# Branch gates of the second block: from two plain tile products to the seven-product scheme, with weight sums made by accumulating DMAs

## What is computed

```python
def hybrid_mixer(h, w_in, w_diff_o, w_sb_o, w_moba_o, w_out, ...):
    proj = h @ w_in                      # h: 256 positions x 1024
    (dq, dk, dv, sq, sk, sv, mq, mk, mv, g_diff, g_sb, g_moba) = jnp.split(proj, offsets, axis=-1)
    a_out = ... diff_attention ...       # softmax, two maps per head
    b_out = ... stick_breaking_attention ...
    c_out = ... moba_attention ...       # softmax
    merged = (jax.nn.sigmoid(g_diff) * (a_out @ w_diff_o)
              + jax.nn.sigmoid(g_sb) * (b_out @ w_sb_o)
              + jax.nn.sigmoid(g_moba) * (c_out @ w_moba_o))
    return merged @ w_out
```

## Time and profile before

| | us |
|---|---|
| median of 3 runs | 3351.42 |
| lowest and highest run | 3348.72, 3353.06 |
| the profiled execution | 3349.66 |
| its span in the trace | 3347.8 |

### The profile page before, as it was taken

The page is one execution under the profiler, slowest core; times in us unless marked ns, Lnnn a source line. Parts: engine busy times, 40 slices in busy tenths (PEclk is TensorE's granted clock), DMA queues, the critical chain, the costliest instruction groups (busy, mean ns, idle before and its releaser), DMA issues.

```text
span 3347.8 us, 54286 instructions
## 1 busy us (share of the span) xinstructions
PE 3288.6 (98%) x22634; PEld 2943.0 (88%) x22634; DVE 2120.8 (63%) x4269; ACT 682.9 (20%) x1675; POOL 187.1 (6%) x140
## 2 busy tenths in 40 slices
PE   7999999999999999999999999999999999999999
PEld 5888755788888888878999999988999999988999
DVE  3579654456654157765789685744486886644685
ACT  2101442012211011242122111124211212032211
POOL 0000000005443400000000000000000000000000
PEclk9999999999999999999999999999999999999999
DMA  6243001223223443503554445633444444633443
GB/s 241 77 176 126 26 26 63 101 87 126 84 84 111 153 150 126 186 32 114 190 187 160 170 166 182 176 132 114 140 175 164 164 169 160 191 125 121 156 164 127
DMA packets 67397, 453.76 MB, mean 136 GB/s; under 512 B 7377, under 2 KB 11857, under 8 KB 15057
## 3 DMA queue, kind: packets, MB, share of 16 engines
q1 hardware_dynamic: 66384, 446.09, 37.7%
q10 hardware_dynamic: 768, 4.20, 0.7%
HBM read 445.02 MB, written 1.05 MB: 133 GB/s over the span
## 4 chain that ended last, share of the span: by engine, by line
PE 91%; DVE 6%; ACT 2%; DMA 1%; issue 1%; SPq 0%; DVEq 0%; ACTq 0%
PE bank L1353 64%; PE bank L1041 14%; DVE conv_sum L2847 3%; PE bank L1666 2%; PE bank L1153 1%; PE bank L1183 1%; PE bank L1106 1%; PE bank L1091 1%; PE bank L1208 1%; PE bank L1713 1%; PE bank L1298 1%; DMA weight_ring<-w_o 1%; PE bank L1276 0%; PE bank L1503 0%; PE bank L1287 0%
## 5 line engine op out<-in xcount | busy, mean ns | idle before, releaser
L1353 PE MATMUL bank<-normed,weight_ring 128*128 128x128 f32 (+1 forms) x5472 | 764.6, 295 | 5.3 <-ACT normed L1883 1.5
L1353 PEld LDWEIGHTS bank<-normed,weight_ring 128*128 128x128 f32 x5472 | 707.7, 192 | 42.4 <-issue 7.6
L1353 PE MATMUL bank<-normed,mixer_small 128*128 128x128 f32 (+1 forms) x3040 | 387.2, 281 | 0.0
L1353 PEld LDWEIGHTS bank<-normed,mixer_small 128*128 128x128 f32 x3040 | 366.4, 192 | 4.9
L1353 PE MATMUL bank<-region_a,weight_ring 128*128 128x128 f32 (+1 forms) x2128 | 294.4, 293 | 0.7 <-DVE region_a L2804 0.6
L1353 PEld LDWEIGHTS bank<-region_a,weight_ring 128*128 128x128 f32 x2128 | 272.1, 192 | 11.7 <-issue 2.0
L1353 PE MATMUL bank<-turned,weight_ring 128*128 128x256 f32 (+1 forms) x944 | 199.0, 353 | 0.0
L1353 PEld LDWEIGHTS bank<-turned,weight_ring 128*128 128x128 f32 x944 | 163.6, 190 | 18.4
L1041 PE MATMUL bank<-turned,weight_ring 128*128 128x256 f32 x768 | 178.8, 382 | 0.0
L1353 PE MATMUL bank<-region_a,mixer_small 128*128 128x128 f32 (+1 forms) x1232 | 161.8, 282 | 0.0
L1041 PEld LDWEIGHTS bank<-turned,weight_ring 128*128 128x128 f32 x768 | 140.8, 190 | 22.5 <-issue 5.0
(11 more groups left out here) (340 smaller groups left out, 4883.8 us busy)
## 6 DMA issues: line engine op xcount, KB each, us to landing
weight_ring<-w_ada SPq DMA_DIRECT2D x48, 1024.0 KB, 5.8
weight_ring<-w_up SPq DMA_DIRECT2D x44, 1024.0 KB, 4.8
weight_ring<-w_f1up SPq DMA_DIRECT2D x44, 1024.0 KB, 4.8
weight_ring<-w_f2up SPq DMA_DIRECT2D x44, 1024.0 KB, 4.8
weight_ring<-w_gt SPq DMA_DIRECT2D x32, 1024.0 KB, 4.8
weight_ring<-w_qk SPq DMA_DIRECT2D x24, 1024.0 KB, 4.8
weight_ring<-w_v SPq DMA_DIRECT2D x20, 1024.0 KB, 5.9
weight_ring<-w_pj SPq DMA_DIRECT2D x16, 1024.0 KB, 4.8
```

Of the source, the lines that this page charges most:

```text
L1353: mm = nc.tensor.matmul(bank[u.bank][:, pair.columns(p)], lhs(k), rhs(k), start=begins and p in pair.opens and k == 0, stop=ends and p in ...
```

## The change

The 24 gate tiles become 12 pairs by the seven-product scheme. Each pair's seven products are dealt to the same four filler halves: products 1 and 2; 7 and 6; 5; 3 and 4. The first two halves fill bank 6, the last two bank 7. ACT no longer copies whole tiles but one quarter of the pair (`gate_first`); DVE puts the pair together in its loop (`gate_mix`, placed behind `exponent` and ahead of `store`) and writes it to `gates2`. Since the weight sums are made by adds alone, the signs of the scheme are moved: the activation sums are partly negated, each pair's second tile comes out negated, and the sigmoid of it is taken with scale -1. The activation sums are four DVE operations ahead of the loop. The weight sums are made by DMAs that POOL issues: one load of three quarters of the block from HBM into an entry of `wsum`, and four adds.

```diff
+GATE_PARTS = [(1, 2), (7, 6), (5,), (3, 4)]
+GATE_PAIRS = 12
@@ PE, a half of a filler
+                    if name == "gt2":
+                        x, n = 2 * (g % 2) + half, GATE_PAIRS * l + g // 2 + 1
+                        if g == 0 and half == 0:
+                            pe.wait_ge(turned_ready, T.next(turned_ready, 4))
+                        if x == 1:
+                            pe.wait_ge(gate_s1_s3, 32 * n)
+                            pe.wait_ge(gate_s2, 16 * n)
+                        if x == 3:
+                            pe.wait_ge(gate_s4, 16 * n)
+                        seven(b, g // 2 % SUM_RING, plan.pairs[name][g // 2], KD // 2, gate_act, None, gsums_used,
+                              True, True, l, wsum, None, None, GATE_PARTS[x], 4, (2, 0, 1))
+                        return
...
-                    if name == "sv2":
-                        mm = value_part(u, b, g % 2, range(half * n, half * n + n))
-                    else:
-                        mm = product(bank[u.bank][:, 0:SEQ], b, g % 2 * KD + half * n, hnorm2, 0, SEQ, n, half * n,
-                                     half == 0, half == 1)
+                    mm = value_part(u, b, g % 2, range(half * n, half * n + n))
@@ ACT
-                def gate_copy(g):
-                    u = plan.units["gt2"][g]
-                    full_bank(u, 0, l)
-                    a_(gates2[g // KD][:, g % KD, :], bank[u.bank][:, 0:SEQ], ACT.Copy).then_inc(bank_free[u.bank], 1)
+                def gate_first(g):
+                    units = plan.units["gt2"]
+                    full_bank(units[g], 0, l)
+                    if g >= 4:
+                        emptied(act, units[g - 4], l)
+                    a_(one_gate[:, g // 2 % 2, :], bank[units[g].bank][:, 0:P], ACT.Copy).then_inc(one_copied, 1)
...
-                        x = gates2[b][:, m:m + n, :]
-                        a_(x, x, ACT.Sigmoid).then_inc(gates2_ready, 1)
+                        x, minus = gates2[b][:, m:m + n:2, :], gates2[b][:, m + 1:m + n:2, :]
+                        a_(x, x, ACT.Sigmoid)
+                        a_(minus, minus, ACT.Sigmoid, scale=-1.0).then_inc(gates2_ready, 1)
@@ DVE, ahead of the loop
+                v.tensor_tensor(minus_t1, b11, b12, ALU.subtract).then_inc(turned_ready, 1)
+                v.scalar_tensor_tensor(minus_t2, minus_t1, -1.0, b22, ALU.mult, ALU.subtract).then_inc(turned_ready, 1)
+                v.tensor_tensor(hn[:, half:KD, P:2 * P], b22, b12, ALU.subtract).then_inc(turned_ready, 1)
+                v.scalar_tensor_tensor(hn[:, 0:half, P:2 * P], minus_t2, -1.0, b21, ALU.mult, ALU.subtract
+                                       ).then_inc(turned_ready, 1)
@@ DVE, in the loop
+                    gate_mix(n - 1)
                     if n >= 1 and n % 2 == 0:
                         store(n // 2 - 1)
...
+                gate_mix(23)
                 store(11)
@@ POOL
+            for l in range(DEPTH):
+                u = plan.units["qk2"][-1]
+                pool.wait_ge(bank_full[u.bank], count(u, 0, l) + 1)
+                for j, b in enumerate(plan.blocks["gt2"]):
+                    n = GATE_PAIRS * l + j + 1
+                    quarters = weights["gt2"][l * N_BLOCKS["gt2"] + j]
+                    a21 = ring_t[:, b.slot * SLOT + 2 * w:b.slot * SLOT + 3 * w]
+                    s2, s4, s1 = (wsum[:, j % SUM_RING, i, :] for i in range(3))
+                    if n > SUM_RING:
+                        pool.wait_ge(gsums_used, n - SUM_RING)
+                    g.dma_start(wsum[:, j % SUM_RING].rearrange("p a c -> p (a c)"), quarters[:, 0:3 * w]
+                                ).then_inc(gate_loaded, 16)
+                    pool.wait_ge(slot_landed[b.slot], (count(b, 0, l) + 1) * 16)
+                    g.dma_start(a21, quarters[:, 0:w], accum_op=ALU.add).then_inc(gate_s1_s3, 16)
+                    pool.wait_ge(gate_loaded, 16 * n)
+                    g.dma_start(s1, quarters[:, 3 * w:4 * w], accum_op=ALU.add).then_inc(gate_s1_s3, 16)
+                    pool.wait_ge(gate_s1_s3, 32 * n)
+                    g.dma_start(s2, s1, accum_op=ALU.add).then_inc(gate_s2, 16)
+                    pool.wait_ge(gate_s2, 16 * n)
+                    g.dma_start(s4, s2, accum_op=ALU.add).then_inc(gate_s4, 16)
```

More of the change, by code:

```diff
@@ L272, in filler2 @@
         self.blocks[name][-1].after = self.units[name][-1]
+        if name == "gt2" and g % 2:
+            self.pairs.setdefault(name, []).append(Pair(self.units[name][-2:], P, False))
     def take_blocks(self, name, dram, n, cols, first=0):
@@ L868, in build @@
         gains_ready, resa_ready = sem("gains_ready"), sem("resa_ready")
+        gsums_used, gate_loaded, gate_s1_s3, gate_s2, gate_s4 = (sem(n) for n in (
+            "gsums_used", "gate_loaded", "gate_s1_s3", "gate_s2", "gate_s4"))
         qk_pair, swap_landed = sem("qk_pair"), [sem(f"swap{i}_landed") for i in range(2)]
@@ L1318, in attention1, with seven @@
                         turn(n + 1)
-            def seven(b, s, pair, n, act, made, used, begins, ends, l=0, ring=wsum, midway=None, behind_first=None, part=None):
+            def seven(b, s, pair, n, act, made, used, begins, ends, l=0, ring=wsum, midway=None, behind_first=None, part=None, had=None, at_=(0, 1, 2)):
                 def quarter(q):
@@ L1335, in seven @@
                 order = part or pair.order
-                waited = 0 if 4 in order else 4
+                waited = had if had is not None else 0 if 4 in order else 4
                 if 1 in order:
@@ L2881, in sums_of @@
                         dve.wait_ge(sums_used, V.next(sums_used))
+                    if x == FFN2:
+                        dve.wait_ge(gsums_used, (l + 1) * GATE_PAIRS)
                     dve.wait_ge(slot_landed[b.slot], (count(b, 0, l) + 1) * 16)
@@ L3258, in halves, with mix_y @@
                     V.sent(turned_ready)
-                def mix_y(j, y, dst):
+                def mix_y(j, y, dst, one=one2):
                     dve.wait_ge(one_copied, V.next(one_copied))
@@ L3265, in mix_y @@
                     v.tensor_tensor(seg[:, 0:2], bank[y.bank][:, P:3 * P].rearrange("p (s c) -> p s c", c=P),
-                                    one2[:, j % 2, :].unsqueeze(1).to_broadcast([P, 2, P]), ALU.add).then_inc(mix_step, 1)
+                                    one[:, j % 2, :].unsqueeze(1).to_broadcast([P, 2, P]), ALU.add).then_inc(mix_step, 1)
                     dve.wait_ge(mix_step, V.at(mix_step, V.sent(mix_step)))
@@ L3453, in layer2, with gate_tiles, gate_mix @@
                         dve.wait_ge(rope_ready, V.at(rope_ready, V.made["rope_ready"]))
+                half = KD // 2
+                b11, b21 = hnorm2[:, 0:half, 0:P], hnorm2[:, half:KD, 0:P]
+                b12, b22 = hnorm2[:, 0:half, P:2 * P], hnorm2[:, half:KD, P:2 * P]
+                minus_t1, minus_t2 = hn[:, 0:half, 0:P], hn[:, half:KD, 0:P]
+                dve.wait_ge(hnorm2_ready, (l + 1) * half)
+                v.tensor_tensor(minus_t1, b11, b12, ALU.subtract).then_inc(turned_ready, 1)
+                dve.wait_ge(turned_ready, V.sent(turned_ready))
+                v.scalar_tensor_tensor(minus_t2, minus_t1, -1.0, b22, ALU.mult, ALU.subtract).then_inc(turned_ready, 1)
+                second = V.sent(turned_ready)
+                v.tensor_tensor(hn[:, half:KD, P:2 * P], b22, b12, ALU.subtract).then_inc(turned_ready, 1)
+                V.sent(turned_ready)
+                dve.wait_ge(turned_ready, second)
+                v.scalar_tensor_tensor(hn[:, 0:half, P:2 * P], minus_t2, -1.0, b21, ALU.mult, ALU.subtract
+                                       ).then_inc(turned_ready, 1)
+                V.sent(turned_ready)
+                def gate_tiles(g):
+                    return gates2[g // KD][:, g % KD:g % KD + 2, :].rearrange("p a c -> p (a c)")
+                def gate_mix(n):
+                    g = n if n % 2 == 0 else n - 1
+                    if not 0 <= g < 24:
+                        return
+                    y, x = plan.units["gt2"][g:g + 2]
+                    if n % 2 == 0:
+                        mix_y(g // 2, y, gate_tiles(g), one_gate)
+                    else:
+                        mix_x(y, x, gate_tiles(g))
                 def scores(n):
```

10 lines of the change are left out of this document (7 added, 3 removed).

## The result

The changed kernel takes 3531.3 us, the median of 4 runs (3526.0 to 3532.7), where the kernel before takes 3350.1 in runs beside them: a ratio of 1.0539, interval 1.0525 to 1.0552. It is 181 us slower; the forecast was 24. The profiled execution took 3525.98 us, its span is 3524.2.

A forecast was written before the change was run, and what follows sets the result against it. PE bounds the kernel before; after the change POOL's chain of DMAs would, at 4.2 + 3.6 + 3.6 + 0.6 = 12.0 us per pair: +12.2 us per layer, +24.4 together, 3376 us, range 3338 to 3409.

The forecast's parts named there:

- The mechanism: Gate loop: POOL's chain of DMAs sets the pace and PE waits for its sums; chance 0.55, at 3376 us.
- the formula: Both layers' gate loops: cost of 2 x (11 C - 119.8) us over the kernel before.
- C: POOL's repeating period per gate pair, load + add + add with the s4 add beside the next load: 12.0 us.
- the upper end of 15.4: POOL's period if each pair meets SP's loads as badly as the loads of w_o do: 11.4 + 4.0 us.
- the lead: Start of the gate loop: first pair's s2 ready at 2205.6, PE asks for it about 2218; 12 us.
- the first rival: Gate loop: POOL's chain stays hidden, its period at most 10.5 us, time 3342 us; chance 0.25.
- The third rival: Gate loop: clock falls in PE's waits, gate matmuls slow, 60 us more, time 3436 us; chance 0.06.
- PE and DVE alone: Gate loop without POOL's waits: PE saves 8.4 us per layer, DVE's chain loses 3.8; 9.2 us won in all.
- lost to the chain: Stick-breaking turns: PE waits for DVE about 1.1 us at n = 16, 18, 20 and 0.5 at 22; 3.8 per layer.
- The Trainium skill's price: POOL's DMAs: 2.0 us each plus bytes at 436 GB/s; load 3.8, add 3.2, period 10.2 us.

The follow-up runs named there:

- the reordered chain: Changed kernel with the next pair's load issued behind this pair's add to s1, the add into the slot behind the add to s2: 3410.4 us, ratio 1.0184.
- without the sums: Changed kernel with POOL's own additions in place of its DMAs, each cut to one column in place of 512: 3340.1 us, ratio 0.9975.
- the pieces: Changed kernel with POOL's own additions in place of its DMAs, each made as four of 128 columns: 3341.4 us, ratio 0.9979.

## Why the prediction was wrong in size

**The mechanism held.** POOL's chain sets the pace, and the next load is issued only behind this pair's s2. With PE's waits in between, the formula gives 3510 for the measured period.

**The step that failed is the size of C**, "4.2 + 3.6 + 3.6 + 0.6 = 12.0". Term by term for the pair shown: the load with the add to s4 ahead of it, 4.8 forecast, 6.8 measured; the add to s1, 3.6 and 6.7; the add to s2, 3.6 and 3.7; the issue between s4 and the load, which I left out, 0.5. Each price was that of a DMA by itself. By itself an add within SBUF does take 3.6, though that a plain transfer of 512 KB on SP's queue took the same is luck; an add from HBM took 4.0 to 4.3. But only the add to s2 runs alone. The add to s1 meets a 1 MB load of SP in every pair behind the first (in ten of the eleven the two are issued within 1.1 us of each other), since both hang on the same event: when s2 lands, PE finishes its pair some 7 us later and frees the slot, and POOL's next load lands after 7 to 8 us too. The row of SP's queue in the pair shown, against POOL's issue at 2261.26:

```profile
2261.13 0.33 SPq L941 DMA_DIRECT2D weight_ring<-w_gt  x1
```

I had named this meeting, as the upper end of 15.4, and chosen against it. By the loads cut to a quarter it is worth 1.6 us of the mean period (18.2 to 16.6), and 2.1 us of the add to s1 in the second to eighth pairs (6.8 to 4.6).

The add into the slot stood in the sum at nothing, without a reason. Left out alone, it gave back 0 and 0.4 us of the period; its price is in the lead, some 14 us for both layers. With SP's short loads and without that add, the period is still 16.3 and 15.9, about 4 above the forecast: the load behind the add to s4 takes some 6.3 in place of 4.8 and the add from HBM mostly 4.1 to 4.8 in place of 3.6, and in the late pairs SP's next loads lie beside them. That the add to s4 lengthens the load is inferred, so the sizes within C are only in part shown.

**The sum that I didn't make.** The earlier trace rows already allowed it: a share of 0.32 over 8.94 us is 2.9 us of the DMA engines per pair for SP's 1 MB. POOL's 768 KB and four adds, counted twice for their two fetches, are 2.75 MB more, 8.0 us by the same rate: 10.9 together, above the 8.2 that PE takes. This estimate would have excluded the first rival, the hidden chain, to which I gave 0.25; it would not have shown 18.2, since it lies under my 12.0. The measured figure, in the reordered chain, is about 12.

**The lead** of 12 us was wrong as well: s2 of the first pair, forecast at 2205.6, landed just before 2216.7, since the first adds met the loads that SP issues every 7 to 8 us from 2193.71 to 2215.48 to fill its four slots. With these loads cut to a quarter the add to s4 behind it is issued at 2206.75 in place of 2216.72. So the 92.4 us of the first layer split into 12.2 forecast, 11.1 of lead, 11 x (18.2 - 12.0) = 68.3 of C, and 0.8 behind the last sum.

**The third rival's mechanism was there, its price was not.** The clock fell, as these windows about one wait show (PE, PEld, DVE, ACT, POOL, clock):

```profile
2282.70:2288.90 6.20, 0.00 (x0) 0.00 (x0) 1.77 (x7) 0.49 (x1) 0.87 (x1) 0.83 0.55 104
2289.00:2291.00 2.00, 2.00 (x9) 2.00 (x10) 0.00 (x0) 0.00 (x0) 1.79 (x3) 0.50 0.20 34
...
2294.00:2296.00 2.00, 2.00 (x20) 2.00 (x18) 0.66 (x3) 0.00 (x0) 0.00 (x0) 1.00 0.95 293
```

Behind 6.2 us without a matmul the granted clock is 0.50, the level of 1.2 GHz, and from 2294 us 1.00 again. My argument against it was that PE would be busy two thirds of the time; it was (133 of 208 us), and the clock fell all the same. But the price of 60 us took the slow matmuls as added time, and most of that runs where PE would wait for POOL: filling the waits gave back some 7.

**PE and DVE alone** were right in sum: 9.2 us forecast, 8.75 measured without the sums. In its first layer the loop ends at 2326.76, forecast 2327.0. The parts were near, too. Pairs at the first softmax heads come 8.29 us apart in place of 8.94, so 0.65 for my 0.70. Three pairs at stick-breaking heads take 0.29 longer than before (10.80 us for 10.51): beside the 0.65 that isn't won, 0.94 each is lost to the chain, forecast 1.1. In the last pair it is 0.43, forecast 0.5. The places are right, three turns with both waits and one with the bank's alone. PE's rows show only part of the loss as waiting, 0.18 for the bank and 0.26 for DVE's link; the run of 8 records that ends in such a wait takes 1.16 us with its drain, where one behind which PE is fed costs 0.89:

```profile
2291.54 1.16 PE L1360 MATMUL bank<-normed,mixer_small 128*128 128x128 f32 x8 [0.18 <-DVE region_o L3302]
2292.96 0.67 PE L1747 MATMUL bank<-region_b,constants 128*128 128x256 f32 x2 [0.26 <-DVE region_b L3558]
```

In the changed kernel itself none of these waits shows; they lie inside the waits for POOL, as forecast.

**The Trainium skill's price** (page "DMA: Bandwidth & Descriptors", anatomy of a DMA by the GpSimd path) had given a load of an estimated 3.8 us and, with an add's two reads, an add of 3.2. Single ones that met little else took 4.6 and 3.6 to 4.3, so here the traces stand above it; it is a price per DMA, as mine was.

## What to carry to other kernels

Before pricing a chain of DMAs link by link, add up how long all queues together hold the DMA engines per step: a share of the kernel before, scaled by bytes, with an add counted at twice its bytes or more. If that exceeds the step's time on the bounding engine, no order hides it. Then ask of each link which other transfer is released by the same event, because those two can meet at every step, as they did here. Where an idle engine can add in place, try that ahead of a transfer that adds: here it was cheaper, and cheaper still in short pieces, since another engine's chain ran beside it.

## What the runs showed of the hardware

- A DMA that adds held the DMA engines about 2.2 times as long as a copy (1.7 against 0.76 us for 256 KB), and having its source in SBUF made it no faster.
- Of the 3.6 us that an add alone took within SBUF, 1.5 are work of the DMA engines. A second DMA beside it can use the rest: the reordered chain had the engines busy 90% of the time, the changed kernel 67%.
- Beside an addition of POOL, DVE's operations with both inputs in SBUF lasted until it ended: 1.35 us (2289.87 to 2291.22, POOL's addition 2289.75 to 2291.07) for one that takes 0.28, while additions with an input in PSUM kept their 0.42. The Trainium skill says this on its page "SBUF — State Buffer", "Who interferes with whom": a vector instruction with two SBUF inputs contends with a GpSimd instruction that reads SBUF, and the contention is an exclusive lock. The traces agree, and the pieces show what follows from it: the same operation took 0.54 us beside a piece.
